# A slot's share of the output projection as one run of eight matmuls instead of two halves, in the attention and in the last stage

## The chip, the core and the metric

The kernel runs on one core of a Trainium2 chip. The metric is the device time of one execution in microseconds (us), from the first to the last instruction of the program. A core has five engines with a queue of their own each: TensorE (PE in the profile, with its weight loads as PEld), VectorE (DVE), ScalarE (ACT), GpSimd (POOL) and SyncE (SP), which here only issues DMAs. Each takes its instructions in order; between engines only semaphores order the work.

## What is computed

One inference step of a hybrid decoder layer for a prompt of 1024 tokens and for 8 sequences of 4 new tokens (32 decode rows). One input projection feeds three groups of heads, and one output projection joins them:

```
u = rmsnorm(x, g_pre);  P = u @ w_in
a = mlstm(P)      # 4 heads x 256, matrix memory, chunkwise
b = dsa(P)        # 4 heads x 128, attention over 256 chosen keys
c = memory(P)     # 4 heads x 128, attention over 256 memory tokens
y = x + rmsnorm(concat(a, b, c) @ w_out, g_post)
```

`w_out` is 2048 x 2048. Its rows 0 to 1023 belong to group a, its rows 1024 to 2047 to b and c. All is float32.

## The kernel before

The program runs in stages: input projection and index scores, selection of the keys, then `attend_bc` (attention of groups b and c) and `mix_out` (the mLSTM of group a and the end). The output projection is split between the last two. `attend_bc` multiplies the b and c part of the heads by the lower half of `w_out` and stores the partial sums to DRAM (`y_part`); `mix_out` multiplies the a part by the upper half, adds the stored partial sums, normalises and writes y.

In both stages the projection of the prompt is cut into 32 groups: eight tiles of 128 tokens by four column blocks of 512 (`O_B` = 4, `O_W` = 512). A group adds eight matmuls (j = 0 to 7, 128 rows of `w_out` each) in one PSUM bank of 128 x 512. `multiply(n, half)` issues four of them: half 0 has the waits in front (the turned heads of the token tile kept, the weights loaded, the bank read), half 1 signals the end. The profile shows each of these float32 matmuls as two records.

Both stages are pipelines over slots, one slot for each unit (token tile or chunk, head), 32 units, written out by hand: each engine has a loop `for s in slots`, and in it the steps stand in a fixed order, each with its waits. A group follows its unit by `A_LAG` = 6 slots in the attention and by `LAG` = 5 in the last stage, so the first slots have no `multiply`, and the last ones have nothing but it.

The order of TensorE in a slot of the attention (lines 2100 to 2124): `turn_p(s-1)` (transposes of the softmax), `dots(s)` (scores of the unit for both kinds of head), `multiply` half 0, `turn_h(s-2)` (transposes of the finished heads, tile `ho`), `mix(s-1)` (probabilities times values, bank `ov`), `turn_m(s)` (two transposes of the memory softmax, bank `qm`), `multiply` half 1, `mix_m(s)` (memory probabilities times values; its weights are `pmT`, which ScalarE's `keep_m` copies from `qm` after `turn_m`, and it also waits for VectorE's `finish`, which reads `ov`), and in 16 slots from slot 6 on `decode` (a quad of the decode rows' sum). The bank `acc` is copied by ScalarE's `evacuate`, and SyncE stores the copy.

The order of TensorE in a slot of the last stage (lines 3061 to 3120): `turn(s+2)` (transposes of keys), `multiply` half 0, `dots(s+1)` (query-key products in the bank `dn`), `turn_h(s-1)` (transposes of the unit's output, tile `a`), `decode(s-1)` (state update of a decode row, with its numerator in every fourth slot), `multiply` half 1, `numerator(s)` (three products into another part of the bank `dn`), `key_values(s)` (the state's update, banks `kv`). `dots` waits with `a_ready` until VectorE's `output` of unit s-1 has read that unit's numerator out of the bank `dn`. Between `numerator` and `output` lie VectorE's `denominator`, ScalarE's `square`, GpSimd's `root` (two small operations) and a multiplication on VectorE. The two `acc` banks are read by VectorE's `scale` (adds the partial sums), followed by `out_square` on ScalarE and `gain_of` on GpSimd.

Of the kernel before, what the change touches and what calls it, by code (L numbers as in the profile page):

```python
# [1747 lines left out]
def attend_bc(k):  # L1748
# [33 lines left out]
    with ExitStack() as st:  # L1782
# [44 lines left out]
        def group(s):  # L1827
            return s - A_LAG if 0 <= s - A_LAG < A_UNITS else None
# [107 lines left out]
        def _(pe):  # L1936
# [68 lines left out]
            def turn_p(s):  # L2005
                pe.wait_ge(p_ready, s + 1)
                if s:
                    pe.wait_ge(kept_a, s)
                    pe.wait_ge(kept_v, wide(s))
                if s >= 2:  # L2010
                    pe.wait_ge(h_kept, s - 1)
                for c in range(width(s) // P):
                    last = nc.tensor.transpose(pt[c // 4][:, c % 4 * P:(c % 4 + 1) * P], p[:, c * P:(c + 1) * P], k.ident[:])
                last.then_inc(p_turned, 1)
# [16 lines left out]
            def multiply(n, half):  # L2031
                t, b = n // O_B, n % O_B
                if half == 0:
                    pe.wait_ge(h_kept, H * (t + 1))
                    pe.wait_ge(w_in[b], 16)
                    if n:
                        pe.wait_ge(evacuated, n)
                for j in range(4 * half, 4 * half + 4):
                    last = nc.tensor.matmul(acc[:, :], hT[:, t % 2, j, :], w[:, j, b * O_W:(b + 1) * O_W], start=j == 0,  # L2039
                                            stop=j == HT - 1)  # L2040
                if half:
                    last.then_inc(bc_done, 1)

            def turn_h(s):
                pe.wait_ge(finished, s + 1)
                pe.wait_ge(m_finished, s + 1)
                pe.wait_ge(kept_v, wide(min(s + 2, A_UNITS)))
                if s:
                    pe.wait_ge(h_kept, s)
                for j in range(2):  # L2050
                    last = nc.tensor.transpose(pt1[:, j * P:(j + 1) * P], ho[:, s % 2, j, :], k.ident[:])
                last.then_inc(h_turned, 1)
# [15 lines left out]
            def turn_m(s):  # L2068
                pe.wait_ge(m_ready, s + 1)
                for c in range(2):  # L2070
                    last = nc.tensor.transpose(qm[:, N_MEM + c * P:N_MEM + (c + 1) * P], pm[:, c * P:(c + 1) * P], k.ident[:])
                last.then_inc(m_turned, 1)
# [27 lines left out]
            for s in slots:  # L2100
                if 1 <= s <= A_UNITS:
                    turn_p(s - 1)
                if s < A_UNITS:
                    dots(s)
                if group(s) is not None:
                    multiply(group(s), 0)
                if 2 <= s <= A_UNITS + 1:
                    turn_h(s - 2)
                if 1 <= s <= A_UNITS:
                    mix(s - 1)  # L2110
                if s < A_UNITS:
                    turn_m(s)
                if group(s) is not None:
                    multiply(group(s), 1)
                if s < A_UNITS:
                    mix_m(s)
                if quad(s) is not None:
                    decode(quad(s))
                if s == FIRST_QUAD + QUADS + 5:
                    pe.wait_ge(od_ready, 1)  # L2120
                    for j in range(HT):
                        last = nc.tensor.transpose(dec[:, j * NS:(j + 1) * NS], od[:, j // H, j % H * DH:(j % H + 1) * DH],
                                                   k.ident[0:NS, 0:NS])
                    last.then_inc(od_turned, 1)
# [285 lines left out]
def mix_out(k):  # L2410
# [39 lines left out]
    with ExitStack() as st:  # L2450
# [41 lines left out]
        def group(s):  # L2492

            return s - LAG if 0 <= s - LAG < UNITS else None
# [466 lines left out]
        def _(pe):  # L2961
# [54 lines left out]
            def multiply(n, half):  # L3016
                c, b = n // O_B, n % O_B
                if half == 0:
                    pe.wait_ge(h_kept, ML_H * (c + 1))
                    pe.wait_ge(w_in[b], 16)  # L3020
                    if n >= 2:
                        pe.wait_ge(scaled, n - 1)
                    elif n == 0:
                        pe.wait_ge(d_sd, 1)
                    else:
                        pe.wait_ge(cols_kept, 2)
                for j in range(4 * half, 4 * half + 4):
                    last = nc.tensor.matmul(acc[n % 2][:, :], hT[:, c % 2, j, :], w[b][:, j, :],  # L3028
                                            start=j == 0, stop=j == HT - 1)
                if half:  # L3030
                    last.then_inc(out_done, 1)
# [29 lines left out]
            for s in slots:  # L3061
                if s + 2 < UNITS:
                    turn(s + 2)
                if s == -2:
                    pe.wait_ge(n_in, 16)
                    for c in range(2):
                        last = nc.tensor.transpose(th[:, c * NS:(c + 1) * NS], nin[:, c * P:(c + 1) * P],
                                                   k.ident[0:NS, 0:NS])
                    last.then_inc(n_turned, 1)
                    pe.wait_ge(d_in, 48)  # L3070
                    for x, bank in ((dq, kv0), (dk, kv1)):
                        for c in range(8):
                            last = nc.tensor.transpose(bank[:, c * NS:(c + 1) * NS], x[:, c * P:(c + 1) * P],
                                                       k.ident[0:NS, 0:NS])
                    last.then_inc(d_turned, 1)
                if s == -1:
                    pe.wait_ge(d_kept, 3)
                    for h in range(ML_H):
                        for c in range(2):
                            last = nc.tensor.matmul(acc0[0:NS, h * NS:(h + 1) * NS], dkT[:, 2 * h + c, :],  # L3080
                                                    dqT[:, 2 * h + c, :], start=c == 0, stop=c == 1)
                    last.then_inc(d_dots, 1)
                    pe.wait_ge(filled, 1)
                if group(s) is not None:
                    multiply(group(s), 0)
                if -1 <= s and s + 1 < UNITS:
                    dots(s + 1)
                if 1 <= s <= UNITS:
                    turn_h(s - 1)
                if decode_step(s) is not None:  # L3090
                    decode(decode_step(s))
                if s == UNITS + 1:
                    for h in range(ML_H):
                        last = nc.tensor.matmul(dnum[NS * h:NS * (h + 1), 0:V1], zero[:, :], dv[0:NS, h, :], start=False,
                                                stop=True, skip_group_check=True)
                    last.then_inc(d_close, 1)
                    pe.wait_ge(c_done, 2 * UNITS)
                    nc.tensor.transpose(tq[0:2 * ML_H, 0:P], state[:, :, :, ML_D].rearrange("p h c -> p (h c)"),
                                        k.ident[:]).then_inc(pn_turned, 1)
                    pe.wait_ge(d_n, DEC)  # L3100
                    for c in range(2):
                        last = nc.tensor.transpose(kv0[0:NS, c * P:(c + 1) * P], nnT[:, c, :], k.ident[:])
                    last.then_inc(dn_turned, 1)
                if s == UNITS + 3:
                    pe.wait_ge(d_a, 1)
                    pe.wait_ge(h_kept, UNITS)
                    for c in range(2):
                        last = nc.tensor.transpose(th[:, c * P:(c + 1) * P], da[:, c * P:(c + 1) * P], k.ident[:])
                    last.then_inc(dh_turned, 1)
                if group(s) is not None:  # L3110
                    multiply(group(s), 1)
                if 0 <= s < UNITS:
                    numerator(s)
                    key_values(s)
                if s == 0:
                    pe.wait_ge(d_sd, 1)
                    pe.wait_ge(dv_in, 32)
                    for h in range(ML_H):
                        nc.tensor.matmul(dnum[NS * h:NS * (h + 1), 0:V1], dsd[:, h * NS:(h + 1) * NS], dv[0:NS, h, :],
                                         start=True, stop=False, skip_group_check=True)  # L3120
# [134 lines left out]
```

## Time and profile before

| | |
|---|---|
| median of 3 runs | 2872.42 us (2871.02 to 2876.4) |
| profiled execution | 2867.35 us, span 2865.6 us |
| TensorE busy | 2754.0 us, 96% of the span |
| VectorE, ScalarE, GpSimd busy | 1255.4, 583.6, 412.1 us |
| chain that ended last, largest line | TensorE L3028 (`multiply` of the last stage), 8% |
| attention with groups in it | from 2082 to 2442 us |
| last stage, slots with groups in it | from 2511 to 2845 us |

Times in the rows are microseconds from the start of the span. A busy time is the sum of the operations of an engine; the granted clock (PEclk) is the share of full clock that TensorE got in a stretch, 1.00 or 0.50 or a mean of the two. In a timeline a row gives the start, the duration, the engine, the line, the operation with the tile that it writes and those that it reads, and how many records it joins; a bracket at the end gives the idle time of the engine ahead of it and what ended that. The end of a TensorE record is modelled; the distance between two starts is the better measure.

### The profile page before, as it was taken

What the parts mean: (1) busy time and instruction counts of PE and PEld (TensorE: products, weight loads), DVE (VectorE), ACT (ScalarE), POOL (GpSimd) and SP (SyncE); (2) the same over time, 40 slices, a digit from 0 to 9 for tenths busy, and PEclk for the clock granted to TensorE, in tenths of its full rate; (3) what the DMA queues carried; (4) which work ended last, traced back from release to release, by engine and by line L of the source; (5) the groups of instructions that cost most, each with busy time, mean ns of one, the idle gap of its engine ahead of it and who ended that gap; (6) DMA issues with size and microseconds to landing.
All of it is one profiled execution on the core that took longest, in us unless ns stands there. A gap on an engine that the chain in (4) does not pass through costs nothing. (4 is left out here: it accounts for less than half of the span.)

```text
span 2865.6 us, 35790 instructions
## 1 busy us (share of the span) xinstructions
PE 2754.0 (96%) x13683; PEld 1954.8 (68%) x13683; DVE 1255.4 (44%) x2165; ACT 583.6 (20%) x1367; POOL 412.1 (14%) x819
## 2 busy tenths in 40 slices
PE   8998999999999999999999999999699999699998
PEld 6674468865854488888888888888555564355553
DVE  3152498767755754132222244441322331345553
ACT  3122457842000000000000100100222221122221
POOL 0000023320000000000000022220133100334341
PEclk9999999999999999999999999999899999699999
DMA  6467202112222311322342354452945214665652
GB/s 234 95 159 237 92 16 88 46 55 81 66 81 70 112 47 61 82 66 87 107 130 70 92 164 143 136 155 91 310 148 156 79 46 134 202 197 174 206 171 79
DMA packets 273301, 341.45 MB, mean 119 GB/s; under 512 B 40956, under 2 KB 226292, under 8 KB 267852
## 3 DMA queue, kind: packets, MB, share of 16 engines
q1 hardware_dynamic: 235932, 259.57, 29.2%
q0 software_dynamic: 16288, 67.46, 7.7%
q10 hardware_dynamic: 20912, 12.14, 1.5%
q8 instruction: 110, 1.80, 0.3%
q14 instruction: 59, 0.48, 0.1%
HBM read 261.64 MB, written 80.01 MB: 119 GB/s over the span
## 5 line engine op out<-in xcount | busy, mean ns | idle before, releaser
L1343 PE MATMUL sbank<-w,xT 128*128 128x256 f32 x3328 | 728.3, 380 | 2.9 <-ACT w L1375 2.9
L1343 PEld LDWEIGHTS sbank<-w,xT 128*128 128x128 f32 x3328 | 631.8, 190 | 92.6 <-ACT w L1375 3.7
L1343 PE MATMUL sbank<-w,area 128*128 128x256 f32 x1664 | 361.3, 379 | 0.0
L1733 DVE TENSOR_TENSOR pout_b<-pout_b,sbank 128x256 f32<-128x256 f32 x320 | 134.3, 421 | 511.2 <-PE sbank L1343 414.2
L1343 PEld LDWEIGHTS sbank<-w,area 128*128 128x128 f32 x1664 | 315.9, 190 | 42.8
L1691 DVE TENSOR_TENSOR w<-w 128x2048 f32<-128x2048 f32 x64 | 145.2, 2289 | 327.2 <-PE sbank L1343 266.7
L1418 ACT ACTIVATE pout_b<-sbank 128x256 f32<-128x256 f32 x128 | 48.0, 382 | 918.6 <-PE sbank L1343 666.5
L2039 PE MATMUL at_bank_bc<-w,at_hT 128*128 128x512 f32 x512 | 230.0, 593 | 3.9 <-ACT at_bc_out L2194 3.9
L1343 PE MATMUL sbank<-w 128*128 128x256 f32 x832 | 181.7, 379 | 0.0
L1343 PEld LDWEIGHTS sbank<-w 128*128 128x128 f32 x832 | 158.1, 190 | 21.5
L1340 PE MATMUL sbank<-xT,w 128*128 128x512 f32 x384 | 166.6, 593 | 0.0
L2039 PEld LDWEIGHTS at_bank_bc<-w,at_hT 128*128 128x128 f32 x512 | 94.6, 190 | 103.0 <-issue 101.6
L1340 PEld LDWEIGHTS sbank<-xT,w 128*128 128x128 f32 x384 | 72.7, 190 | 90.1 <-issue 90.0
L3028 PE MATMUL mo_bank_acc<-area,w 128*128 128x512 f32 x256 | 116.7, 600 | 0.0
L3028 PE MATMUL mo_bank_acc<-w 128*128 128x512 f32 x256 | 116.2, 598 | 0.0
L1441 ACT ACTIVATE pout_b<-pout_b 128x256 f32<-128x256 f32 x72 | 30.0, 417 | 358.9 <-DVE pout_b L1733 352.8
L1930 POOL DMA_INDIRECT at_vg<-in_cache_v,rowid x64 | 60.5, 945 | 277.3 <-PE at_bank_dec L2092 144.8
L1340 PE MATMUL sbank<-area,w 128*128 128x512 f32 x192 | 82.9, 592 | 0.0
L3028 PEld LDWEIGHTS mo_bank_acc<-area,w 128*128 128x128 f32 x256 | 46.7, 191 | 52.9 <-issue 52.9
L3028 PEld LDWEIGHTS mo_bank_acc<-w 128*128 128x128 f32 x256 | 46.5, 190 | 52.1 <-issue 52.0
L1516 DVE MAX8 m8s<-decode_scores 128x8 f32<-128x2052 f32 x32 | 73.4, 2293 | 0.1
L1519 DVE FIND_INDEX8 c8s<-m8s,decode_scores 128x8 uint32<-128x2052 f32 x32 | 73.3, 2290 | 0.0
(439 smaller groups left out, 3302.2 us busy)
## 6 DMA issues: line engine op xcount, KB each, us to landing
w<-in_w_in SPq DMA_DIRECT2D x64, 1024.0 KB, 5.3
proj<-pout_b SPq DMA_DIRECT2D x208, 128.0 KB, 1.7
area<-in_x_prompt SPq DMA_DIRECT2D x16, 1024.0 KB, 7.4
attention_then_units<-proj SPq DMA_DIRECT2D x128, 128.0 KB, 2.6
area<-roped_q_of_decode POOLq DMA_DIRECT2D x32, 256.0 KB
w<-in_w_out SPq DMA_DIRECT2D x4, 2048.0 KB, 16.0
y_of_groups_b_c<-at_bc_out SPq DMA_DIRECT2D x32, 256.0 KB
out_sample_C<-mo_dec_states SPq DMA_DIRECT2D x32, 256.0 KB, 3.1
```

The source lines that it names most:

```text
L1340: last = nc.tensor.matmul(bank[2 * u][:, :], at[name][:, c, P * u:P * (u + 1)], x(c, 0, SEQ // 2), start=first_ and c == 0, stop=c == 7, s ...
L1343: last = nc.tensor.matmul(bank[t][:, 0:256], x(c, t * P, (t + 1) * P), at[name][:, c, :], start=first_ and c == 0, stop=c == 7, skip_group ...
L1418: nc.scalar.activation(out[:, t, :], product_at(n, t), function if kind else ACT.Copy).then_inc(first_read, 1)
L1441: nc.scalar.activation(qout[:, t, :], qout[:, t, :], function).then_inc(shaped, 1)
L1516: order.step(nc.vector.max(m8s[:], ss[:]))
L1519: order.step(nc.vector.max_index(c8s[:], m8s[:], ss[:]))
L1691: nc.vector.tensor_tensor(quarter[out], quarter[x], quarter[y], op).then_inc(w_sums, 1)
L1733: nc.vector.tensor_tensor(out[:, t, :], x[:, t, :], product_at(n, t), ALU.add).then_inc(sums_read, 1)
L1930: nc.gpsimd.indirect_dma_start(out=vg[:, 4 * (q % 2) + g, :], out_offset=None, in_=ins["cache_v"][:, :], in_offset=bass.IndirectOffsetOnAx ...
L2039: last = nc.tensor.matmul(acc[:, :], hT[:, t % 2, j, :], w[:, j, b * O_W:(b + 1) * O_W], start=j == 0, stop=j == HT - 1)
L3028: last = nc.tensor.matmul(acc[n % 2][:, :], hT[:, c % 2, j, :], w[b][:, j, :], start=j == 0, stop=j == HT - 1)
```

## The change

Both halves of a group are issued one right after the other. In the attention the second half moves up to the first, ahead of `turn_h`, `mix` and `turn_m`. In the last stage the first half moves down to the second, behind `dots`, `turn_h` and `decode`. Nothing else changes: the waits inside `multiply(n, 0)` and the signal inside `multiply(n, 1)` go with them, and the other engines' programs are the same.

```diff
@@ attend_bc, tensor @@
                 if group(s) is not None:
                     multiply(group(s), 0)
+                    multiply(group(s), 1)
                 if 2 <= s <= A_UNITS + 1:
                     turn_h(s - 2)
                 if 1 <= s <= A_UNITS:
                     mix(s - 1)
                 if s < A_UNITS:
                     turn_m(s)
-                if group(s) is not None:
-                    multiply(group(s), 1)
                 if s < A_UNITS:
                     mix_m(s)
@@ mix_out, tensor @@
                     pe.wait_ge(filled, 1)
-                if group(s) is not None:
-                    multiply(group(s), 0)
                 if -1 <= s and s + 1 < UNITS:
                     dots(s + 1)
...
                 if group(s) is not None:
+                    multiply(group(s), 0)
                     multiply(group(s), 1)
                 if 0 <= s < UNITS:
                     numerator(s)
```

## Rows read from the trace of the kernel before

**Rows 1.** Busy time by stretch: length, each engine's busy time, PEclk, DMA share, GB/s

```profile
2150.00:2380.00 230.00, 230.00 (x989) 133.09 (x987) 74.49 (x192) 66.56 (x152) 30.47 (x33) 1.00 0.29 88
...
2523.00:2800.00 277.00, 276.76 (x1050) 155.66 (x1049) 145.75 (x410) 59.15 (x177) 108.36 (x184) 1.00 0.60 184
```

**Rows 2.** Timeline of one attention slot with a group: start, us, engine, line, operation

```profile
2233.68 0.38 PE L2071 MATMUL at_bank_mem<-ident_sb,at_pm 128*128 128x128 f32 x2
...
2233.90 3.60 PE L2039 MATMUL at_bank_bc<-w,at_hT 128*128 128x512 f32 x8
...
2233.95 0.35 DVE L2330 SCALAR_TENSOR_TENSOR at_ho<-at_bank_pv,at_rr,area 128x128 f32<-128x128 f32 x1 [2.36 <-issue]
...
2234.10 0.38 ACT L2188 ACTIVATE at_pmT<-at_bank_mem 128x256 f32<-128x256 f32 x1 [0.95 <-PE at_bank_mem L2071]
```

**Rows 3.** Timeline of attention slots ahead of the first group

```profile
2062.41 0.44 PE L2071 MATMUL at_bank_mem<-ident_sb,at_pm 128*128 128x128 f32 x2 [1.00 <-ACT at_pm L2164]
...
2062.88 0.38 ACT L2188 ACTIVATE at_pmT<-at_bank_mem 128x256 f32<-128x256 f32 x1
...
2063.32 0.71 PE L2081 MATMUL at_bank_pv<-at_mv,at_pmT 128*128 128x128 f32 x4 [0.47 <-ACT at_pmT L2188]
...
2074.13 0.44 PE L2071 MATMUL at_bank_mem<-ident_sb,at_pm 128*128 128x128 f32 x2 [0.86 <-ACT at_pm L2164]
...
2075.66 0.71 PE L2081 MATMUL at_bank_pv<-at_mv,at_pmT 128*128 128x128 f32 x4 [1.10 <-ACT at_pmT L2188]
```

**Rows 4.** Timeline of one last-stage slot, from dots to dots

```profile
2570.47 0.61 PE L2977 MATMUL mo_bank_dots_num<-attention_then_units,mo_kT 128*128 128x128 f32 x4
...
2576.70 1.03 PE L3002 MATMUL mo_bank_kv<-attention_then_units,mo_kw 128*128 128x257 f32 x4
...
2577.57 0.38 PE L2967 MATMUL mo_bank_turn_qk<-ident_sb,attention_then_units 128*128 128x128 f32 x2
...
2577.78 3.60 PE L3028 MATMUL mo_bank_acc<-w 128*128 128x512 f32 x8
...
2577.93 0.47 ACT L2785 ACTIVATE mo_hjunk<-mo_bank_dots_num,mo_small 128x256 f32<-128x256 f32 x1 [6.22 <-DVE mo_small L2604]
...
2579.88 0.48 DVE L2613 SCALAR_TENSOR_TENSOR mo_a<-mo_bank_dots_num,mo_small,mo_gg 128x256 f32<-128x256 f32 x1
...
2581.22 0.61 PE L2977 MATMUL mo_bank_dots_num<-attention_then_units,mo_kT 128*128 128x128 f32 x4
```

**Rows 5.** Timeline of last-stage slots ahead of the first group

```profile
2496.09 0.68 PE L2977 MATMUL mo_bank_dots_num<-attention_then_units,mo_kT 128*128 128x128 f32 x4 [1.50 <-DVE mo_a L2613]
...
2503.36 0.48 DVE L2613 SCALAR_TENSOR_TENSOR mo_a<-mo_bank_dots_num,mo_small,mo_gg 128x256 f32<-128x256 f32 x1
...
2503.99 0.68 PE L2977 MATMUL mo_bank_dots_num<-attention_then_units,mo_kT 128*128 128x128 f32 x4 [2.10 <-DVE mo_a L2613]
```

**Rows 6.** Busy time by stretch, as rows 1, with the granted clock

```profile
98.00:106.00 8.00, 5.38 (x82) 3.39 (x81) 3.70 (x4) 1.70 (x5) 0.55 (x1) 1.00 0.24 48
...
2060.00:2080.00 20.00, 12.02 (x75) 9.16 (x74) 10.22 (x40) 9.29 (x34) 0.00 (x0) 1.00 1.05 386
...
2488.00:2494.50 6.50, 6.50 (x18) 4.17 (x17) 2.52 (x9) 1.19 (x4) 1.43 (x5) 0.50 0.88 294
...
2494.90:2497.80 2.90, 1.72 (x11) 1.25 (x12) 1.76 (x6) 0.89 (x3) 2.27 (x5) 1.00 0.76 230
...
2498.20:2501.40 3.20, 3.20 (x9) 2.46 (x8) 1.39 (x6) 0.00 (x0) 0.00 (x0) 0.50 0.56 178
...
2501.70:2504.70 3.00, 0.90 (x8) 0.69 (x6) 2.10 (x5) 1.01 (x4) 2.50 (x5) 1.00 0.57 164
...
2505.10:2511.60 6.50, 6.50 (x17) 4.37 (x16) 3.62 (x16) 1.16 (x4) 0.94 (x4) 0.50 0.39 112
```

**Rows 7.** Timeline of slot 32 of the last stage, TensorE

```profile
2807.28 1.03 PE L3002 MATMUL mo_bank_kv<-attention_then_units,mo_kw 128*128 128x257 f32 x4
...
2811.58 0.38 PE L3013 MATMUL mo_bank_turn_h<-ident_sb,mo_a 128*128 128x128 f32 x2
```


## The prediction

> **What bounds the kernel now.** I began with the busy time by stretch, since the change touches two stages and a mean over the whole span would mix them. In the slots of the attention that hold a projection group, and in those of the last stage, TensorE is busy 230.00 of 230.00 us and 276.76 of 277.00 us, at a granted clock of 1.00, while of the other engines none is busy more than 53% of either stretch (VectorE, 145.75 of 277.00 us) [rows 1]. So both stages are bound by TensorE alone: no wait of it is left that a new order could remove, and every wait that a new order adds is paid in full. Then I read the timeline of one slot of each stage in order to see what the two halves of `multiply` hide. One half is four matmuls of 128x512, eight records of about 0.43 us: the half that starts at 2577.78 holds TensorE until 2581.22, so 3.44 us [rows 4].
>
> Last I looked at the slots that run ahead of the first group (lag 6 in the attention, lag 5 in the last stage). They issue the same operations with no `multiply` among them, so the trace of before already shows the waits bare [rows 3, 5].
>
> **The amount of work** doesn't change: 32 groups of eight matmuls in either stage, the same operands, banks and semaphores, no DMA and no instruction on another engine. Only the place of four matmuls of each group changes. SP, ScalarE, VectorE and GpSimd keep their own order. The accumulator's copy or addition still follows the group's last matmul: at the same place of the slot in the last stage, and earlier in the attention, where that hides as before.
>
> **Attention: the second half moves up, away from between `turn_m` and `mix_m`.** `mix_m` takes as weights what ScalarE copies out of the bank that `turn_m` has just filled. Now turn_m starts at 2233.68 and the second half at 2233.90; ScalarE's copy runs 2234.10 to 2234.48, and VectorE's `finish`, for which mix_m waits too, 2233.95 to 2234.30, both wholly under the 3.44 us of matmuls [rows 2]. After the change mix_m is next in the queue at 2233.90 and can start about when the copy has ended: with the 0.06 us by which the bare case follows its copy (2062.88 + 0.38 = 2063.26, then 2063.32 [rows 3]), at 2234.54, thus 0.64 us late. The bare slots give a second price for this: turn_m at 2062.41 and mix_m at 2063.32 are 0.91 us apart, against 0.22 us where nothing has to be waited for, so 0.69 us [rows 2, 3]. The dearest bare slot is 1.53 us apart (2074.13 to 2075.66), 1.31 us late [rows 3]; there ScalarE was still busy with the softmax of its slot. I take 0.67, because in the changed slot the softmax of both heads has eight matmuls of cover ahead of turn_m, not four, and ScalarE stands idle when turn_m ends. Behind mix_m are queued the decode quad and the next slot's transposes; all of them move by the same time. The wait exists only where a group and a mix_m meet, slots 6 to 31: 26 x 0.67 = 17.4 us (bounds 26 x 0.64 = 16.6 and 26 x 1.31 = 34.1). `turn_m`'s own wait, for the softmax of the memory branch, is covered by eight matmuls instead of four, but nothing was paid for it before. In slots 32 to 37 the accumulator's copy is hidden once more and once less than now; I cost that at nothing. The clock: bare slots with two waits each in every 4 us still ran at 1.00 from 2060 to 2080 [rows 6], so I expect no fall here.
>
> **Last stage: the first half moves down, from ahead of `dots` to ahead of `numerator`.** `dots(s+1)` and `numerator(s)` share one bank. So dots must wait until VectorE has read the numerator of unit s-1 out of it (`output`, tile mo_a), and turn_h transposes that same tile. This is a long chain over four engines: numerator done, scaled q and three small operations of VectorE, ScalarE's square (2577.93), GpSimd's mean and power, two operations of VectorE, the last from 2579.88 to 2580.36 [rows 4]. In the bare slot dots begins 0.15 us after the end of that operation (2503.36 + 0.48 = 2503.84, then 2503.99) [rows 5]. From the start of key_values at 2576.70 this gives 2580.51, so 3.81 us, and TensorE has 1.08 us of work in that time: key_values and turn, up to 2577.78 [rows 4]. The first half covers the other 2.73 us, and ends only 0.71 us after the chain. Without it TensorE stands still for 3.81 - 1.08 = 2.73 us in each slot. The bare slots did just this, with 1.50 and 2.10 us of idle time that the profile puts down to mo_a [rows 5]; there the clock was at its lower level and key_values itself took twice the time, which is why the idle part is shorter. The rest of the chain isn't touched: scale, square and gain of the finished group keep their places.
>
> By slots: 5 to 29 have turn and dots, 25 x 2.73 = 68.3 us. Slot 30 has no turn (0.21 us less of cover, 2577.57 to 2577.78 [rows 4]): 2.94. Slots 31 and 32 have neither; there turn_h is the first to wait, and comes 4.30 us after the start of key_values (2807.28 to 2811.58 [rows 7]), of which key_values itself fills 0.87 [rows 4]: 2 x 3.43 = 6.9. Sum 78.1 us. Behind dots stand turn_h, the decode step, the eight matmuls, numerator and key_values, so the whole slot moves. What waits on VectorE, ScalarE and GpSimd for these has slack. In exchange the weights (sd) have eight matmuls ahead of numerator instead of four, where nothing was waited for.
>
> **The clock of TensorE** is the other half of the sum. In this stage it fell three times ahead of the first group: after the 1.50 us before 2496.09 the records of 2498.20 to 2501.40 are at 0.50, after the 2.10 us before 2503.99 those of 2505.10 to 2511.60 are, and after a wait for a DMA those of 2488.00 to 2494.50 [rows 5, 6]. The level 0.50 is 1.2 GHz, 1.00 is 2.4 GHz. The idle time that I expect in each slot is longer than the first two. In these three stretches of at least 3.2, 6.5 and 6.5 us TensorE did half the work, so 1.6, 3.25 and 3.25 us were lost, 2.7 us in the mean. What follows the new idle time (dots, turn_h, decode, then dense matmuls) is what follows in those slots too. 28 slots x 2.7 = 75.6 us. Bounds: nothing, if the clock holds, and 28 x 3.25 = 91 us. Against the upper end speaks the one idle time of 2.62 us (8.00 - 5.38) at full clock that no fall followed, between 98 and 106 us [rows 6].
>
> The Trainium skill speaks against this term. TensorE: Matmul & The Clock Gate, section "Why this matters for your kernels", warns of idle gaps between bursts of matmuls only when they are longer than the ones expected here; by that advice the clock would stay up, and the term would be nothing. The rows of this stage disagree, with falls after 1.50 and 2.10 us.
>
> **The sum** is 17.4 + 78.1 + 75.6 = 171 us. The profiled execution took 2867.35 us (span 2865.6); the median of the runs is 2872.42, 0.2% more, and I add the sum to the median: 3043.5 us, 6.0% slower. About 0.2% is what a measurement of this kernel can tell from no change.
>
> **Rivals.** (a) *The clock holds* in the last stage: 17.4 + 78.1, so 2968 us. For it speaks the stretch at 98 to 106 us; against it the three falls in the very stage. It may also fall in a part of the slots only, for instance if slot and clock come into step; then 2975 to 3012. This is the page's advice as a mechanism of this kernel. (b) *The chain gets shorter when it is alone*: in the bare slot, with nothing of scale and out_square between, the steps aren't quicker than in the full one (0.48 us for the last in both [rows 4, 5]), so I give it little. If half of the wait went, 39 us with no fall of the clock, the time would be 2929. (c) *Not slower*: the chain would have to end within the 1.08 us that key_values and turn cover, and the copy of turn_m within 0.22 us. From that point on there is no wait, and joining the halves could save the few hundredths of a microsecond that a change of operand shapes costs, so 2866 to 2872. The chain is 3.81 us long, 2.7 us over the point that decides. (d) *Another wait comes on top*: the dearest bare price in the attention (34 us in place of 17) with the full clock term (91 us): 3076.
>
> **How the numbers follow.** The forecast (falls in nearly every slot, 3012 to 3072) 0.68; clock falls in a part of the slots 0.14; clock holds 0.10; shorter chain 0.05; not slower 0.01; beyond 3072, 0.02. The range 2985 to 3072 leaves out the last four and the lower part of the second, together 0.2. Slower by over 0.2%: 0.98; within 0.2%: 0.01; faster: 0.01.
>
> **What would show it.** In the profile after: mix_m waits for ScalarE's copy in all 32 slots, some 0.5 us of idle each; dots waits for mo_a in about 28 slots at nearly 2.7 us, turn_h in two at over 3 us; one slot of the last stage goes from 10.75 us (dots to dots, 2570.47 to 2581.22 [rows 4]) to 15 to 17 us; the granted clock over the last stage is 0.8 or less, and 1.00 over the attention. If the clock stays at 1.00 in the last stage, the slot is 13.5 us and (a) is right. If dots shows no idle time, the chain was read wrongly. If the attention grows by more than 34 us, another wait than the copy decides there.

## The result and the profile after

The changed kernel takes 3035.43 us (median; 3022.14 to 3058.75) against 2872.52 us: ratio 1.0572, 95% interval 1.0544 to 1.0600, 163 us slower. The profiled execution is the slowest of the five, 3058.75 us with a span of 3057.0 us, 191 us longer than that of before, so its rows below show somewhat more than the median lost.

The page after, busy tenths in 40 slices of the span. The last stage with its groups takes the last seven slices, and has lost both busy time and clock there:

```profile
PE   8998899999999999999999999978999968888887
PEclk9998899999999999999999999999999977878788
```

Who waited for whom on TensorE after, over the whole span (us in total, times, longest):

```profile
PE mo_bank_dots_num L2976 <- DVE mo_a L2612: 72.0, 29, 2.9
PE at_bank_pv L2081 <- ACT at_pmT L2187: 17.2, 32, 1.1
...
PE mo_bank_turn_h L3012 <- DVE mo_a L2612: 6.6, 2, 3.5
```

These are the waits of the forecast: dots and turn_h for mo_a, mix_m for at_pmT. The change brought no other. Before, the waits for mo_a were 4.7 us in 3 times, and mix_m's wait for the copy (at_pmT) 4.5 us in 6 times, all ahead of the first group.

Now both stages from the start of the first matmul of a group to the start of the last, attention and last stage, before:

```profile
2081.90:2434.10 352.20, 348.31 (x1404) 192.51 (x1403) 92.62 (x251) 92.17 (x216) 52.92 (x56) 1.00 0.36 110
2510.80:2844.30 333.50, 333.23 (x1228) 182.65 (x1227) 163.99 (x452) 66.21 (x197) 120.21 (x199) 1.00 0.56 171
```

and after (length, busy time of TensorE, weight load, VectorE, ScalarE, GpSimd, then the granted clock):

```profile
2088.00:2459.10 371.10, 354.97 (x1405) 193.42 (x1403) 92.68 (x251) 90.63 (x216) 53.07 (x56) 1.00 0.33 103
2538.40:3035.80 497.40, 426.15 (x1205) 217.60 (x1201) 161.25 (x446) 64.99 (x194) 117.46 (x194) 0.81 0.38 113
```

The attention grew by 18.9 us at full clock. The last stage grew by 163.9 us in this execution: TensorE was idle 71 us of it (497.40 - 426.15), where it had been idle 0.3 us, and its busy time grew by 92.9 us for the same work, since the clock was 0.81. The other 8.6 of the 191.4 us lie outside these two stretches, 6.1 of them ahead of the attention's first group, where both programs are the same.

One attention slot after, beside [rows 2] of before:

```profile
2240.22 0.38 PE L2071 MATMUL at_bank_mem<-ident_sb,at_pm 128*128 128x128 f32 x2
2240.64 0.38 ACT L2187 ACTIVATE at_pmT<-at_bank_mem 128x256 f32<-128x256 f32 x1 [0.95 <-PE at_bank_mem L2071]
2241.08 0.71 PE L2081 MATMUL at_bank_pv<-at_mv,at_pmT 128*128 128x128 f32 x4 [0.47 <-ACT at_pmT L2187]
2241.72 1.06 PE L2092 MATMUL at_bank_dec<-at_vg,at_p_spread 128*32 128x512 f32 x8
```

mix_m starts 0.86 us after turn_m. The operation behind turn_m started after 0.22 us before, so mix_m is 0.64 us late. mix_m itself then takes 0.64 us to the next operation.

One slot of the last stage after, beside [rows 4]: end of key_values and turn, VectorE's output, dots, turn_h, the decode step, the run of eight, and the next dots:

```profile
2616.96 1.03 PE L3001 MATMUL mo_bank_kv<-attention_then_units,mo_kw 128*128 128x257 f32 x4
...
2617.83 0.38 PE L2966 MATMUL mo_bank_turn_qk<-ident_sb,attention_then_units 128*128 128x128 f32 x2
2620.15 0.48 DVE L2612 SCALAR_TENSOR_TENSOR mo_a<-mo_bank_dots_num,mo_small,mo_gg 128x256 f32<-128x256 f32 x1
2620.78 1.08 PE L2976 MATMUL mo_bank_dots_num<-attention_then_units,mo_kT 128*128 128x128 f32 x4 [2.57 <-DVE mo_a L2612]
...
2623.37 9.28 PE L3027 MATMUL mo_bank_acc<-area,w 128*128 128x512 f32 x16
...
2637.61 0.87 PE L2976 MATMUL mo_bank_dots_num<-attention_then_units,mo_kT 128*128 128x128 f32 x4 [2.56 <-DVE mo_a L2612]
```

From key_values to dots it is 3.82 us (forecast 3.81), of which 2.57 are idle. The slot, dots to dots, is 16.83 us long; it was 10.75. Its clock:

```profile
2617.90:2620.70 2.80, 0.31 (x3) 0.07 (x1) 2.58 (x8) 1.96 (x6) 1.73 (x4) 1.00 0.54 148
2621.00:2627.40 6.40, 6.40 (x15) 3.24 (x15) 1.34 (x4) 0.38 (x1) 2.12 (x3) 0.50 0.76 177
2628.00:2637.40 9.40, 7.04 (x23) 3.89 (x21) 3.10 (x10) 1.96 (x6) 1.63 (x4) 1.00 0.34 110
```

The clock is full while TensorE waits, half from about when it works again, and full for the rest of the run of eight. In this execution every one of the 28 slots with a wait has such a stretch; it begins between 0.1 us before and 0.9 us after the start of the operation that waited (here 2620.78).

### The profile page after: what moved, and what is told of

Same layout as the page of the kernel before. It is cut to its first block and busy times, and to the rows that moved or that the text cites. A ratio compares the mean times of both kernels' runs of the same rounds, so it can differ in the third digit from the quotient of the medians.

```text
span 3057.0 us, 35790 instructions
## 1 busy us (share of the span) xinstructions
PE 2858.3 (94%) x13683; PEld 1994.1 (65%) x13683; DVE 1254.7 (41%) x2165; ACT 582.3 (19%) x1367; POOL 413.2 (14%) x819
## 5 line engine op out<-in xcount | busy, mean ns | idle before, releaser
L1343 PEld LDWEIGHTS sbank<-w,xT 128*128 128x128 f32 x3328 | 632.6, 191 | 92.9 <-ACT w L1375 3.7
L3027 PE MATMUL mo_bank_acc<-w 128*128 128x512 f32 x256 | 147.4, 741 | 0.0
L3027 PE MATMUL mo_bank_acc<-area,w 128*128 128x512 f32 x256 | 140.9, 713 | 0.0
L3027 PEld LDWEIGHTS mo_bank_acc<-w 128*128 128x128 f32 x256 | 60.1, 242 | 84.1 <-issue 74.9
L2583 DVE TENSOR_TENSOR mo_qs<-attention_then_units 128x256 f32<-128x256 f32 x32 | 13.8, 432 | 237.0 <-PE mo_bank_dots_num L2990 174.0
L3027 PEld LDWEIGHTS mo_bank_acc<-area,w 128*128 128x128 f32 x256 | 57.9, 233 | 80.9 <-issue 76.3
L2976 PE MATMUL mo_bank_dots_num<-attention_then_units,mo_kT 128*128 128x128 f32 x128 | 28.0, 354 | 72.2 <-DVE mo_a L2612 72.0
L2784 ACT ACTIVATE mo_hjunk<-mo_bank_dots_num,mo_small 128x256 f32<-128x256 f32 x32 | 15.2, 474 | 368.0 <-DVE mo_small L2603 368.0
```

Source lines behind the costliest of these rows:

```text
L1343: last = nc.tensor.matmul(bank[t][:, 0:256], x(c, t * P, (t + 1) * P), at[name][:, c, :], start=first_ and c == 0, stop=c == 7, skip_group ...
L2976: last = nc.tensor.matmul(dots_at, kT[:, n % 2, c, :], q[:, n % 4, c, :], start=c == 0, stop=c == 1)
```

## The experiments

They ask four things: do the two parts add; are wait and clock two costs, and does the idle time cause the second; is it the run of eight that costs, or its place; and is it VectorE's chain that is waited for.

The ratio compares with executions of before taken beside the run (their medians are 2870.86, 2872.97 and 2872.85 us); a share of time in the text is this ratio, times 2872.5 us.

| kernel | median us | ratio to before, 95% |
|---|---|---|
| attention_only | 2893.87 | 1.0068 (1.0047 to 1.0090) |
| last_stage_only | 3009.06 | 1.0495 (1.0454 to 1.0537) |
| last_stage_wait_filled | 2960.05 | 1.0308 (1.0284 to 1.0332) |
| last_stage_eight_first | 2883.08 | 1.0035 (1.0025 to 1.0046) |
| last_split_3_5 | 2880.73 | 1.0035 (1.0022 to 1.0048) |
| last_split_2_6 | 2903.89 | 1.0115 (1.0085 to 1.0144) |
| last_split_1_7 | 2948.76 | 1.0266 (1.0242 to 1.0289) |
| attention_split_7_1 | 2873.39 | 0.9994 (0.9982 to 1.0007) |
| last_stage_shorter_chain | 2999.10 | 1.0445 (1.0424 to 1.0465) |
| eight_first_loads_ahead | 2875.02 | 1.0003 (0.9990 to 1.0016) |
| attention_eight_second | 2884.24 | 1.0032 (1.0016 to 1.0048) |

### attention_only and last_stage_only: one part of the change each

> The attention's part of the change alone: the second half moves up to the first, the last stage is as before. Theory (a copy of ScalarE laid bare, 0.67 us in 26 slots, clock at 1.00): 17.4 us more than before, 2890 us, and mix_m waits for ScalarE's copy in 32 slots. Rival (the clock of TensorE falls in the attention too): 30 us or more, with a granted clock below 1.00 between 2150 and 2400 us. Rival (something else hides it): within 5 us of before.

> The last stage's part alone: the first half moves down to the second, the attention is as before. Theory (78 us of waiting for mo_a and 60 to 75 us of lost clock): what the whole change cost less 17 us, so 3005 to 3025 us, dots waiting 2.6 to 2.9 us in each slot, granted clock 0.80 in the stage. Rival (the two parts don't add, since the second takes up waits of the first): under 3000 or over 3035 us.

The edits are the first and the second half of the change's diff. The attention's part costs 0.68%, 19.5 us, and the last stage's 4.95%, 142 us; the sum is 5.63%, within the interval of the whole (5.44 to 6.00%). The attention alone, by stretch as above:

```profile
2088.70:2460.50 371.80, 355.66 (x1404) 193.71 (x1403) 92.64 (x251) 90.58 (x216) 52.91 (x56) 1.00 0.33 103
```

The stage is 19.6 us longer than before. The clock is 1.00, so the rival with a falling clock is out for it. The 19.5 us are 2 more than 26 x 0.67. The slot shows where: mix_m to the next operation takes 0.64 us after the wait; before it was 0.54 (2237.34 to 2237.88), and in the split with one matmul left in between (attention_split_7_1), where mix_m doesn't wait either, it is 0.53 (2241.83 to 2242.36). So a slot loses 0.64 + 0.1 us, and 26 such are 19 us.

### last_stage_wait_filled: something to do in the wait

```diff
@@ mix_out, tensor; the last stage's part of the change, and @@
             def multiply(n, half):
...
-                if half == 0:
+                if not half:
...
-                for j in range(4 * half, 4 * half + 4):
+                for j in range(4 * half, 4 * half + 4) if half is not None else range(3):
...
-                                            start=j == 0, stop=j == HT - 1)
+                                            start=j == 0, stop=j == HT - 1 or half is None and j == 2)
...
+                if group(s) is not None:
+                    multiply(group(s), None)
                 if -1 <= s and s + 1 < UNITS:
                     dots(s + 1)
```

> The last stage's part, with the first three matmuls of each group issued at the old place as well (their sums are written over when the group's run of eight begins; nothing that is stored changes). TensorE then has 2.58 us of work in the 2.7 us in which it would wait. Theory (wait and clock are two costs, and the idle time is what makes the clock fall): clock at 1.00, dots waits some 0.15 us, and the time is before + 32 x 2.58 us + small rests, 2955 to 2965 us, 50 to 65 us less than with the wait empty although TensorE has more to do. Rival (the clock falls for another reason, such as the order of the operations, or its fall costs nothing beyond the wait): not faster than the kernel with the wait empty, 3010 us or more.

2960.05 us, 49 us faster than with the wait empty (3009.06), although 32 x 3 matmuls, 83 us of work, were added that nobody needs. A slot of it, from turn over the three matmuls to dots:

```profile
2605.14 0.38 PE L2967 MATMUL mo_bank_turn_qk<-ident_sb,attention_then_units 128*128 128x128 f32 x2
2605.36 2.74 PE L3028 MATMUL mo_bank_acc<-w 128*128 128x512 f32 x6
2608.09 0.68 PE L2977 MATMUL mo_bank_dots_num<-attention_then_units,mo_kT 128*128 128x128 f32 x4
...
2609.55 7.13 PE L3028 MATMUL mo_bank_acc<-w 128*128 128x512 f32 x16
2616.52 0.60 PE L2989 MATMUL mo_bank_dots_num<-attention_then_units,mo_sd 128*128 128x257 f32 x2
```

dots comes 0.15 us later than the three matmuls alone would let it, as forecast, and the run of eight that took 9.28 us above takes 7.13. From the first to the last matmul of a group no stretch of low clock is left (ahead of it there are still some):

```profile
2508.50:2931.50 423.00, 421.08 (x1420) 216.80 (x1419) 163.76 (x453) 66.74 (x199) 120.61 (x200) 1.00 0.45 135
```

So the clock's share is a cost of its own, and it is the idle time that brings it: the order of all the other operations is that of last_stage_only.

### last_stage_eight_first and eight_first_loads_ahead: the run of eight at the other place

```diff
@@ mix_out, tensor, against before @@
                 if group(s) is not None:
                     multiply(group(s), 0)
+                    multiply(group(s), 1)
                 if -1 <= s and s + 1 < UNITS:
                     dots(s + 1)
...
-                if group(s) is not None:
-                    multiply(group(s), 1)
```

> The last stage with its run of eight at the other place: the second half moves up to the first, ahead of dots; the attention is as before. Theory (the place costs, not the run of eight): dots is covered by 6.9 us, and behind it turn_h and decode give VectorE's weights about 1 us, which the trace of before shows to be just enough (weights end at 2582.15, numerator could start at 2582.61), so within 6 us of before, 2867 to 2879 us, clock 1.00. Rival (a run of eight in itself costs): over 2950 us. Rival (the weights or the state update now come late): 10 to 30 us more.

2883.08 us, 0.35% more than before: the run of eight as such doesn't cost 142 us; its place does. But 10 us are over the expected 6. TensorE's waits in this kernel, in the slots with a group (2515 to 2857 us) alone:

```profile
PE mo_bank_turn_qk L2967 <- DMA attention_then_units<-gate_rows: 4.7, 4, 2.1
PE mo_bank_kv L3002 <- DVE mo_dec_states L2669: 1.0, 6, 0.2
```

turn waits for the rows of its unit, 4 times here (8 times and 12.7 us with those ahead of the first group), and key_values for the decode state's update. A slot shows why the rows are late (SPq is SyncE issuing a DMA):

```profile
2715.15 0.17 DVE L2672 COPY mo_nnT<-mo_dec_states 128x2 f32<-128x2 f32 x1
...
2715.35 0.39 SPq L2541 DMA_DIRECT2D out_sample_C<-mo_dec_states  x1
...
2715.78 0.51 SPq L2546 DMA_DIRECT2D mo_dec_states<-in_state_mlstm_C  x1
2716.59 0.62 SPq L2398 DMA_DIRECT2D attention_then_units<-mlstm_queries_turned  x1
...
2718.16 0.44 PE L2967 MATMUL mo_bank_turn_qk<-ident_sb,attention_then_units 128*128 128x128 f32 x2 [1.60 <-DMA attention_then_units<-gate_rows]
```

The decode step now stands behind all eight matmuls, so SyncE, which waits for it, issues the state's store and load (256 KB each) right ahead of a unit's loads. The longest of these waits is also the one place of this stage where the clock fell, for 3.4 us from 2765.0 on:

```profile
2764.90 0.44 PE L2967 MATMUL mo_bank_turn_qk<-ident_sb,attention_then_units 128*128 128x128 f32 x2 [2.12 <-DMA attention_then_units<-gate_rows]
```

So a wait for a DMA can bring a fall as well as one for VectorE. The next run puts the unit's loads first in SyncE's queue:

```diff
@@ mix_out, sync, on top @@
+                if 0 <= s and s + 4 < UNITS:
+                    sp.wait_ge(kv_done, s + 1)
+                    sp.wait_ge(gg_ready, s + 1)
+                    units.load(sp, s + 4)
                 m = decode_step(s)
                 if m is not None:
...
-                if 0 <= s and s + 4 < UNITS:
-                    sp.wait_ge(kv_done, s + 1)
-                    sp.wait_ge(gg_ready, s + 1)
-                    units.load(sp, s + 4)
```

> The last stage's run of eight at the first place, and in SyncE's queue the loads of the next unit ahead of the store and load of a decode state. With the eight first, decode comes late in the slot, SyncE waits for it, and the trace shows 8 waits of turn for the unit's rows, 12.7 us, against 2 and 4.6 us before. Theory (that queue is all of the 10 us that this place costs): at most 2 or 3 such waits within the slots that have a group, and 2868 to 2876 us, as before. Rival (the loads are late because the DMA queues are shared, whatever the order): 2880 us or more again.

2875.02 us, the same as before (1.0003). In the slots with a group no wait of turn for a DMA is left; the only one, 3.2 us long, is ahead of them, at 2496.70. The stage by stretch, first the eight first as such (8.7 us longer than the 333.50 of before), then with the loads ahead:

```profile
2514.90:2857.10 342.20, 336.52 (x1229) 182.30 (x1227) 162.07 (x452) 66.41 (x199) 120.36 (x200) 1.00 0.54 168
```

```profile
2523.10:2858.00 334.90, 333.92 (x1229) 182.38 (x1227) 162.56 (x452) 66.22 (x197) 120.31 (x200) 1.00 0.55 172
```

So one run of eight at the first place costs nothing in the last stage, once SyncE's queue follows. Neither version is faster than before.

### last_split_3_5, last_split_2_6, last_split_1_7: less cover, step by step

```diff
@@ mix_out, tensor, against before; k = 3, 2, 1 @@
-                for j in range(4 * half, 4 * half + 4):
+                for j in range(*((0, k), (k, 8))[half]):
```

> Last stage only: three matmuls of a group at the first place and five at the second, the attention as before. Three matmuls are 2.58 us, the chain leaves 2.73 us to cover, so theory (the wait is what the cover lacks): 0.15 us of waiting for mo_a in 28 slots, 4 us in all, clock at 1.00, 2872 to 2880 us. Rival (every matmul moved behind dots costs its share of the whole loss, a quarter of 140 us): 2900 us or more.

> Last stage only: two matmuls of a group at the first place and six at the second. Two are 1.72 us, so 1.0 us of waiting in 28 slots is 28 us, and a little over 2 us more for slots 30 to 32. Theory (an idle time of 1.0 us in a slot of 11.8 us leaves the clock up): 2900 us, 2896 to 2908. Rival (any idle time of this length makes the clock fall, as after 1.50 us ahead of the first group): up to 75 us more, 2930 to 2980 us.

> Last stage only: one matmul of a group at the first place and seven at the second. 2.73 less 0.86 leaves 1.87 us of waiting in 28 slots, 52 us, and 4 us more in slots 30 to 32. Theory (the clock falls at this length, as it did after 1.50 and 2.10 us ahead of the first group): 55 us and 45 to 75 us of lost clock, 2970 to 3000 us. Rival (the clock holds up to 2 us of idle time): 2924 to 2932 us.

The last stage by stretch, first to last matmul of a group, in the splits 3|5, 2|6, 1|7 and 0|8 (last_stage_only):

```profile
2510.60:2851.00 340.40, 338.48 (x1228) 180.37 (x1227) 163.60 (x452) 66.30 (x197) 120.57 (x200) 1.00 0.55 168
```

```profile
2511.40:2879.50 368.10, 342.40 (x1229) 181.49 (x1227) 163.72 (x453) 66.74 (x199) 120.63 (x200) 0.99 0.51 155
```

```profile
2517.20:2926.00 408.80, 360.56 (x1227) 187.80 (x1227) 163.46 (x452) 66.10 (x197) 120.28 (x199) 0.94 0.47 140
```

```profile
2510.90:2983.70 472.80, 401.68 (x1205) 210.04 (x1201) 161.50 (x446) 64.91 (x194) 117.36 (x194) 0.85 0.40 119
```

Idle time (length less busy time) is 1.9, 25.7, 48.2 and 71.1 us: 22 to 24 us for each matmul taken from the cover, nearly 28 x 0.86. That is the wait, and it is linear. The busy time grows by 5, 9, 27 and 68 us over the 333.2 of before: that is not. Read in steps of 0.25 us from the first to the last matmul of a group, the stretches at low clock in these executions are (waits as counted from the starts; the profile lists each 0.17 us shorter):

```
split   waits of    stretches at 0.50   at 0.50 in all
3|5     0.15 us     none                0 us
2|6     1.0 us      2                   7 us
1|7     1.9 us      13                  45 us
0|8     2.7 us      27                  139 us
after   2.7 us      28                  188 us
```

The two stretches of 2|6 don't belong to the waits of 1.0 us. Each follows the wait of turn_h in one of the two last slots, 31 and 32, where neither turn nor dots covers anything:

```profile
2829.87 0.44 PE L3013 MATMUL mo_bank_turn_h<-ident_sb,mo_a 128*128 128x128 f32 x2 [1.75 <-DVE mo_a L2613]
2843.27 0.44 PE L3013 MATMUL mo_bank_turn_h<-ident_sb,mo_a 128*128 128x128 f32 x2 [1.40 <-DVE mo_a L2613]
```

So no slot with a wait of 1.0 us lost clock, and 2903.89 us for 2|6 is what the wait gives, but for 3.4 us. 2948.76 us for 1|7 lies between its two theories: the clock falls, but in 12 of the 28 slots (the first of the 13 stretches is the end of a fall that began ahead of the first group), and mostly for 3.4 us, so the theory was too high by 21 us at its lower end, and the rival too low by 17 at its upper. Its slots up to 29 have the same wait, listed with 1.7 us, and 10 of the 12 falls follow such a wait; why in these slots and not in the others isn't shown. 3|5 came out 8 us over before where 4 were expected: its slots are 10.98 us (2569.97 to 2580.95), 0.23 over 10.75. Dots starts 0.15 us late, and takes 0.51 to 0.52 us to turn_h where it took 0.44 (2581.22 to 2581.66 before).

### attention_split_7_1 and attention_eight_second: the cover in the attention

```diff
@@ attend_bc, tensor, attention_split_7_1 against before @@
-                for j in range(4 * half, 4 * half + 4):
+                for j in range(*((0, 7), (7, 8))[half]):
@@ attend_bc, tensor, attention_eight_second against before @@
-                if group(s) is not None:
-                    multiply(group(s), 0)
                 if 2 <= s <= A_UNITS + 1:
                     turn_h(s - 2)
...
                 if group(s) is not None:
+                    multiply(group(s), 0)
                     multiply(group(s), 1)
```

> Attention only: seven matmuls of a group at the first place, one left between turn_m and mix_m, the last stage as before. One matmul is 0.86 us, the bare wait was 0.64 to 0.67 us. Theory (the wait for ScalarE's copy is all that the attention's part costs): no wait for the copy in the slots with a group, the same time as before within 5 us. Rival (moving work ahead of turn_h costs something else as well, VectorE or the store of the accumulator): 10 us or more over before.

> Attention only: the whole run of eight at the second place, between turn_m and mix_m; the last stage as before. The wait for ScalarE's copy of the memory softmax is covered, but nothing stands between dots and turn_h any more. Theory (waits follow the cover, step by step): turn_m waits for the exponential of the memory scores where mix is short (0.4 to 0.7 us in the slots of the second and third tile, none in the last tiles), and mix may wait for the copies of turn_p, 5 to 15 us in all, 2877 to 2888 us. Rival (all that counts is the copy behind turn_m): 2868 to 2876 us.

One matmul, 0.86 us, left between turn_m and mix_m takes the whole cost away: 2873.39 us, ratio 0.9994; from the first to the last matmul of a group the stage takes 352.4 us, before 352.2. A slot of it:

```profile
2240.75 0.38 PE L2071 MATMUL at_bank_mem<-ident_sb,at_pm 128*128 128x128 f32 x2
2240.97 1.02 PE L2039 MATMUL at_bank_bc<-w,at_hT 128*128 128x512 f32 x2
2241.17 0.38 ACT L2188 ACTIVATE at_pmT<-at_bank_mem 128x256 f32<-128x256 f32 x1 [0.95 <-PE at_bank_mem L2071]
...
2241.83 0.61 PE L2081 MATMUL at_bank_pv<-at_mv,at_pmT 128*128 128x128 f32 x4
```

The copy ends at 2241.55, and mix_m comes when the matmul is through. With all eight at the second place the other wait opens, that of turn_m for the exponential, by 0.64 us of idle time in the first three slots with a group and some 0.4 us in the next ones, 4.5 us in 12 slots, and the stage is 8.8 us longer than before (361.0 us). The kernel takes 2884.24 us, 0.32% more (0.16 to 0.48%), within the 5 to 15 us of the theory. The waits listed are half of that; where the rest goes wasn't looked for.

### last_stage_shorter_chain: the chain itself

```diff
@@ mix_out, vector, on top of last_stage_only @@
-                    if s + 1 < UNITS and s >= 1:
-                        scaled_q(s + 1)
...
                     if 1 <= s <= UNITS:
                         denominator(s - 1)
+                    if s + 1 < UNITS and s >= 1:
+                        scaled_q(s + 1)
```

> The last stage's part of the change (first half moved down), and VectorE's steps of a slot in another order: denominator(s-1) ahead of scaled_q(s+1), which takes 0.42 us off the chain from numerator to mo_a. Theory (TensorE waits for this chain and for nothing else): each wait for mo_a is 0.4 us shorter, 29 slots, 12 us, with a little lost clock less; against 3009 us for this part alone 2980 to 3000 us, and the waits for mo_a 60 to 66 us in all, not 76. Rival (the wait is for the unit's loads, or set by GpSimd): no change within 5 us of 3009.

2999.10 us, 10 us less than last_stage_only by the medians and 14 by the ratios (4.45% and 4.95%). Its waits for mo_a, in dots and in turn_h:

```profile
PE mo_bank_dots_num L2977 <- DVE mo_a L2613: 59.8, 28, 2.5
...
PE mo_bank_turn_h L3013 <- DVE mo_a L2613: 6.6, 2, 3.5
```

These are 66.4 us against the 69.8 + 6.6 = 76.4 us of last_stage_only. From the first to the last matmul of a group:

```profile
2517.20:2974.10 456.90, 395.64 (x1205) 204.94 (x1201) 156.66 (x446) 64.16 (x194) 117.43 (x194) 0.86 0.41 123
```

That is 15.9 us less than the 472.80 of last_stage_only: 9.9 us of idle time and 6.0 us of busy time, at a clock of 0.86 against 0.85. (The stage began 6.3 us later in this execution, so the whole span is only 9.6 us shorter.) A shorter chain is a shorter wait, microsecond for microsecond, with some clock on top: TensorE waits for this chain.

## Why the prediction was right

**The bound** and the two places were read rightly: no other wait came up, and what was taken from the cover of a chain turned into idle time of TensorE nearly one for one (22 to 24 us for each matmul of 28 x 0.86 us).

**Attention**, forecast 17.4 us: 19.5 us measured (interval 13 to 26). The delay of mix_m was 0.64 us, the lower of the two prices in the prediction and the one of the slot itself. What the term lacked is 0.1 us in a slot: after the wait mix_m takes 0.64 us to the next operation instead of 0.54.

**The wait of the last stage**, forecast 78.1 us: 69.8 + 6.6 = 76.4 us of waits in last_stage_only and 72.0 + 6.6 = 78.6 after. (A few of them lie ahead of the first group; on the other hand each is listed 0.17 us short, 2.57 for 3.82 - 1.08 = 2.74, since a record's end is modelled late.) The chain was 3.82 us for 3.81. The same small price of a restart, 0.08 us (0.52 against 0.44 from dots to turn_h), comes on top. The bare slots ahead of the first group carried this reading. For slots 31 and 32 the reading was wrong and its number right by luck: the 4.30 us from key_values to turn_h in slot 32 before are 0.86 us and the first half's 3.44 us, a distance set by the cover and not by the chain. The chain itself is longer there than 3.81 us, 4.49 and 4.14 us (here key_values to turn_h in slot 32 of last_stage_only):

```profile
2940.14 1.03 PE L3002 MATMUL mo_bank_kv<-attention_then_units,mo_kw 128*128 128x257 f32 x4
2944.28 0.69 PE L3013 MATMUL mo_bank_turn_h<-ident_sb,mo_a 128*128 128x128 f32 x2 [3.11 <-DVE mo_a L2613]
```

**The clock**, forecast 75.6 us as 28 falls of 2.7 us: near in sum, and by luck, since two errors nearly cancel. A fall can be dearer than 2.7 us (6.8 us at half clock, 3.4 us lost, in all 28 slots of the profiled execution, 94 us in all, over the forecast's upper bound of 91), and in other executions not every one is that long: in last_stage_only stretches of 3.4 and 6.8 us follow each other, two and two, and the other four executions of the changed kernel lost 22 to 35 us less to the clock than the profiled one, by their mean clocks. In the median run of the changed kernel the mean clock over the span is 0.957 and the span 3033.7 us, which is 0.043 x 3033.7 = 130 us lost; before it is 0.978 (the median of 50 executions) over 2870 us, 63 us. The difference, some 67 us (a mean clock is given to a thousandth, 3 us), is the clock's share of 163. The two waits with their restarts explain 98 us (19.5 + 76.4 + 28 x 0.08), so the two parts make 165. In the profile the last stage ran at 0.81, and at 0.85 in last_stage_only, where the forecast named 0.8 or less. The term that was mis-sized is the mean of 2.7 us over three stretches ahead of the first group, applied to all 28 slots.

**The rivals.** (a), the clock holds: wrong at 2.7 us of idle time, right at 1.0 us and partly right at 1.9, as the splits show. The Trainium skill's advice (TensorE: Matmul & The Clock Gate, section "Why this matters for your kernels"), that only longer gaps than these cost clock, doesn't hold here: with waits of 1.9 us 13 stretches at 0.50 were seen, with waits of 2.7 us 27 and 28, and nearly all of these waits are shorter than those of which it warns. (b) and (c) gave nothing: the chain is no shorter when it is alone (3.82 us). (d) didn't come. Against "not slower": the same run of eight at the first place is as fast as before.

## What to carry to other kernels

In a stage whose engine is full, work between a producer and its consumer is cover, and has to be counted in microseconds against the length of the chain on the other engines: 3.2 matmuls in the last stage, 0.8 in the attention. What is over may be moved freely (7|1 in the attention, eight at the first place in the last stage, once SyncE's queue followed), what is under is paid one for one, and longer waits are paid once more in clock (here not at 1.0 us in a slot, in fewer than half of the slots at 1.9, in nearly all at 2.7). Before such a move, read the slots in which the cover is missing anyway, at the pipeline's start: they show the bare waits, and the clock behind them.

## What the runs showed of the hardware that was not expected

- The price of a wait isn't its length alone: the records behind it took 0.08 us (dots to turn_h 0.52 us for 0.44) and 0.1 us (mix_m to the next operation 0.64 us for 0.53) more than in a full queue. Both were read at full clock, in last_split_3_5 and in the attention after.
- The clock makes equal executions differ: the five runs of the changed kernel took 3058.75, 3037.67, 3033.96, 3035.43 and 3022.14 us at mean clocks of 0.950, 0.957, 0.958, 0.957 and 0.961. Between the slowest and the fastest, span times lost clock is 152.9 and 117.8 us, so 35 of the 37 us are clock. Why one execution falls for 6.8 us in every slot and another for 3.4 us in some wasn't tried.
- The dose is steep: waits of 1.0, 1.9 and 2.7 us in a slot of 11 to 13.5 us without the fall gave 0, 45 and 139 us at half clock (the 7 us of the split 2|6 follow its two longer waits, listed with 1.75 and 1.40 us).
- Two DMAs of 256 KB, issued in SyncE's queue just ahead of a unit's loads, made turn wait 4 times, 4.7 us, in slots where nothing was waited for with the loads ahead of them.
